# Attention over pairs of heads: VectorE copies turned rows two steps later

## The reference, cut to what matters

```
# "fox" half, per head: causal softmax with a decay added to the logits
logits = q k^T * scale + cum_q - cum_k
p = masked_softmax(logits, causal);  o = p @ v
# "latent" half, per head: softmax over the keys that an index picked
p = masked_softmax(logits, valid);   o = p @ c_sel
```

## Time and profile before

| what | value |
|---|---|
| median of 3 runs | 1916.68 us (1914.93 to 1918.02) |
| profiled execution, its own time | 1919.38 us |
| its span from first to last instruction | 1917.6 us |
| mean granted TensorE clock | 0.988 |
| PE busy | 1839.3 us (96% of the span) |
| DVE busy | 1027.5 us (54%) |
| ACT busy | 828.2 us (43%) |
| POOL busy | 592.6 us (31%) |
| the loop of the change | about 808 to 892 us of the span |

### The profile page before, as it was taken

The page is one execution under the profiler, slowest core; times in us unless marked ns, Lnnn a source line. Parts: engine busy times, 40 slices in busy tenths (PEclk is TensorE's granted clock), DMA queues, the critical chain, the costliest instruction groups (busy, mean ns, idle before and its releaser), DMA issues.

```text
span 1917.6 us, 27389 instructions
## 1 busy us (share of the span) xinstructions
PE 1839.3 (96%) x10554; PEld 1451.5 (76%) x10554; DVE 1027.5 (54%) x2006; ACT 828.2 (43%) x1569; POOL 592.6 (31%) x421
## 2 busy tenths in 40 slices
PE   8999999997888999999999999999999999999998
PEld 7878889842223778767888888889888888888886
DVE  3170442521111869663477676842577725767677
ACT  4123651311111543375554544353377655444543
POOL 4344431011110233356322223233055643232221
PEclk9999999999999999999999999999999999999999
DMA  7223404699999412121132223222203012233321
GB/s 236 98 94 118 140 1 154 251 392 419 420 420 370 167 45 88 46 88 35 54 132 88 88 88 120 98 94 67 45 2 89 2 44 88 88 131 108 113 88 45
DMA packets 86867, 252.06 MB, mean 131 GB/s; under 512 B 12212, under 2 KB 19700, under 8 KB 74448
## 3 DMA queue, kind: packets, MB, share of 16 engines
q1 hardware_dynamic: 81344, 238.79, 33.9%
q0 software_dynamic: 4592, 9.30, 1.3%
q10 hardware_dynamic: 800, 2.20, 0.3%
HBM read 241.89 MB, written 15.73 MB: 134 GB/s over the span
## 4 chain that ended last, share of the span: by engine, by line
PE 86%; DVE 4%; DMA 4%; ACT 3%; issue 2%; POOL 0%; ACTq 0%; DVEq 0%; POOLq 0%
PE psA L1606 42%; PE psS L2054 4%; PE psA L1649 3%; DMA ring<-in_w_down_e 3%; PE psA L2018 2%; PE psO L2352 2%; PE psO L1836 2%; PE psT L1836 2%; PE psS L1836 2%; PE psT L2402 2%; DVE x L3089 2%; DMA big<-in_w_down_e 1%; PE psA L1471 1%; PE psA L1785 1%; PE psS L1649 1%
## 5 line engine op out<-in xcount | busy, mean ns | idle before, releaser
L1290 POOL TENSOR_TENSOR w_slot<-ring,w_slot 128x1024 fp32r<-128x1024 f32 (+1 forms) x81 | 214.0, 2656 | 524.7 <-ACT w_slot L2433 524.4
L1606 PE MATMUL psA<-hT_hi,w_slot 128*128 128x512 f32 x960 | 298.2, 390 | 0.0
L2433 ACT ACTIVATE w_slot<-ring 128x1024 fp32r<-128x1024 f32 (+2 forms) x183 | 196.8, 1086 | 164.4 <-DVE ring L3089 75.0
L1606 PEld LDWEIGHTS psA<-hT_hi,w_slot 128*128 128x128 f32 x960 | 180.4, 188 | 37.3
L1606 PE MATMUL psA<-hT_lo,w_slot 128*128 128x512 f32 x480 | 187.0, 390 | 0.0
L3089 DVE TENSOR_TENSOR w_slot<-ring,w_slot 128x1024 fp32r<-128x1024 f32 x98 | 119.9, 1225 | 115.7 <-ACT w_slot L2433 115.7
L3089 DVE TENSOR_TENSOR x<-psA,x 128x512 f32<-128x512 f32 (+1 forms) x186 | 117.1, 662 | 104.2 <-PE psA L1606 68.8
L1606 PE MATMUL psA<-w_slot,hid_part 128*128 128x512 f32 x672 | 161.4, 390 | 0.0
L2433 ACT ACTIVATE big<-psA 128x512 f32<-128x512 f32 (+6 forms) x134 | 61.7, 482 | 208.7 <-PE psA L1606 126.0
L1606 PEld LDWEIGHTS psA<-w_slot,hid_part 128*128 128x128 f32 x672 | 126.2, 188 | 26.1
L2433 ACT ACTIVATE scr<-scr,stat 128x384 f32<-128x384 f32 (+3 forms) x224 | 123.7, 555 | 19.1 <-DVE stat L4079 9.8
(11 more groups left out here) (557 smaller groups left out, 4450.2 us busy)
## 6 DMA issues: line engine op xcount, KB each, us to landing
ring<-in_mlp_w SPq DMA_DIRECT2D x32, 2048.0 KB, 8.1
ring<-in_w_in SPq DMA_DIRECT2D x8, 2048.0 KB, 8.1
ring<-in_w_gate_e SPq DMA_DIRECT2D x14, 1024.0 KB, 16.3
ring<-in_w_up_e SPq DMA_DIRECT2D x14, 1024.0 KB, 20.7
ring<-in_w_down_e SPq DMA_DIRECT2D x13, 1024.0 KB, 28.3
big<-in_w_down_e SPq DMA_DIRECT2D x12, 1024.0 KB, 26.4
ring<-in_ab_w_in SPq DMA_DIRECT2D x5, 2048.0 KB, 8.6
scr<-in_w_down_e SPq DMA_DIRECT2D x7, 1024.0 KB, 27.0
```

The costliest lines, as they stand in the source:

```text
L1290: nc.gpsimd.tensor_tensor(part(w_lo, c), raw_piece(c), part(w_hi, c).bitcast(F32), ALU.subtract)\
L1606: ins = pe.matmul(o, a, b, start=(at == 1), stop=(at == 3 * len(terms)))
L2433: return nc.scalar.activation(o, i, f, **kw)
```

## The change

DVE copies item i - 8 at odd step i, where it copied item i - 6. The copy stays behind the maximum and the reciprocal of its step. So between the turn of an item and its copy DVE now does both maxima of the next pair and their step's reciprocal, too. No instruction is added or taken away, and ACT's, PE's and POOL's orders stay as they are.

```
--- before.py
+++ after.py
@@ -3937,7 +3937,7 @@
                             scalar=3e38, op0=ALU.add, op1=ALU.min, accum_out=negm[:, col:col + 1]).then_inc(p_masked, 1)
                     if 2 <= i < n_pairs and i % 2:
                         weigh_pair(i)
-                    k = i - TURN_LAG - 1
+                    k = i - TURN_LAG - 3
                     if 0 <= k < n_pairs and k % 2:
                         dve.wait_ge(p_turned, k + 1)
                         if k >= TURNED:
```

## The result

The changed kernel is slower: 1932.64 us median (1931.17 to 1933.81, 4 runs) against 1917.35 us (1914.93 to 1918.14, 4 runs) on the same chip. The ratio is 1.0081, its 95% interval 1.0064 to 1.0099. That is 15.3 us more, where 11.1 were forecast: inside the stated range, but above the forecast's own range of 8.0 to 13.5 added.

A forecast was written before the change was run, and what follows sets the result against it. PE was taken to bound the loop, DVE costing only where PE waits for it. Terms 9.0 + 1.1 + 0.6 + 0.4 = 11.1 us on the 1916.7 us median gave 1927.8 us, range 1923 to 1933.

The forecast's parts named there:

- the forecast's own range: Whole kernel: 8.0 to 13.5 us added to the median, so 1924.7 to 1930.2 us; the forecast had 80%.
- What bounds the kernel: Loop: PE sets the end; DVE's 25.8 us of waits cost nothing by themselves, PE's 1.4 us for copies matter.
- The wait moves to the maximum: DVE in the loop: the first maximum waits for the same turn through its 7-row ring, so the wait stays.
- Item 7's term: Behind item 7's turn (512 columns): PE's next turn comes 1.29 us later in 7 places, 9.0 us.
- Items 3 and 5: Behind their turns, latent half only: 0.27 and 0.14 us lost, four times each, 1.1 and 0.6 us.
- The rival in which the fox half hides the loss: Loop: the turn stalls in the latent half alone, 6.9 us added, 1923.6 us; chance 6%.
- The clock: Loop: PE's stalls make its clock fall, 1.7 us each; three falls taken, 1932.9 us; chance 7%.
- The range: Whole kernel: 1923 to 1933 us, from the stall in the latent half alone to three falls of the clock.
- The rule on VectorE: Item 7's maxima: the next operation waits for an empty pipeline, 1.1 us more in seven places; not counted.
- No change: Behind the loop: the delay is taken up later by a PE wait, 1916.7 us; chance 4%.
- faster: Loop: maxima reach ACT and POOL 0.6 us earlier, PE's waits of 5.0 and 1.4 vanish, 1910.3 us; chance 3%.

The follow-up runs named there:

- The run with eight rows: The changed kernel with 8 instead of 7 SBUF rows for the masked scores: 1922.74 us against 1916.56 before, ratio 1.0030.
- the swap: The changed kernel with a maximum's two waits in the other order, first the turn, then the scores: 1930.24 us against 1916.56 before, ratio 1.0068.
- the filled kernel: The changed kernel with TensorE repeating the narrow pair's scores three times in six steps: 1928.26 us against 1916.56 before, ratio 1.0065.
- the kernel before, filled: The kernel before the change with the narrow pair's scores repeated three times in the same six places: 1918.90 us against 1916.51, ratio 1.0011.

## Why the prediction was right in its mechanism and short in its size

**What bounds the kernel** was right. DVE's 25.8 us of waiting were worth nothing, and PE's 1.4 us were the line to follow. The loss went through to the end: the loop's 15.5 us and the median's 15.3 agree. How often the clock fell in the loop of the timed runs isn't known, so the agreement is good to a fall or two (1.6 us each).

**The wait moves to the maximum** was right: 34.3 us now stand at L3935. The run with eight rows shows that it is the ring of 7 rows that puts it there.

**Item 7's term** (7 x 1.29 = 9.0) was right from the release on, 2.13 us as worked out. It missed 0.11 us ahead of the release, in T itself. I set the maximum's start equal to the copy's, but the maximum waits for two semaphores, the later one last, and starts 0.11 later than the copy did. That is 0.11 in each of 15 places, 1.6 us; the swap took 1.5 us from the loop beside the clock. **Items 3 and 5** (0.27 and 0.14) show the same: PE waits 0.30 and 0.16 there, and the whole latent cycle grew from 8.63 to 887.92 - 877.35 = 10.57 us, so by 1.94 for 1.70 forecast. The fox cycle grew from 831.60 - 821.75 = 9.85, release to release, to 831.21 - 819.95 = 11.26, so by 1.41, where 1.29 + 0.11 is 1.40. The rival in which the fox half hides the loss is out. The sum without the clock would have been 11.1 + 1.6 = 12.7; the runs give 12.3.

**The clock** was the step that failed in weight. I gave it 7% as a rival beside the forecast, on the ground that PE stays much busier here (8.3 of 10.3 us) than around the stalls of the earlier trace rows. That ground failed: the first fall came in a stretch of 8.63 busy us in 10, behind one wait of 1.37 us. It fell twice in the profiled execution, 3.2 us, and these were at nothing in the sum; 11.1 + 1.6 + 3.2 = 15.9, for 15.5 measured. That the falls come from the idle time rests on the kernels side by side: the filled kernel has none, nor has any kernel with shorter waits. Its price for one fall (1.7 us) was good: 1.6 here. The rule of the Trainium skill that I cited (TensorE: Matmul & The Clock Gate, A second HAM failure mode: psum-queue depth-cycling) is borne out by these runs (a granted clock of 0.83, then 0.93 and 0.90, where the loop stood at 1.00 before), and I should have given it more weight, since I weighed it against stalls of 0.34 us in the loop, and the stalls of my own forecast (1.29 us more) were up to five times as long.

**The range** held by luck as much as by the sum. The forecast by itself ended at 1930.2, and the measured 1932.64 lies beyond it. It is inside the stated 1923 to 1933 only because I had stretched that to the rival's three falls, 5.1 us; in their place came two falls and the hand-over, 3.2 + 1.6 = 4.8 us.

The rule on VectorE (VectorE: DVE Perf Modes, The DRAIN you can't avoid) would not have given the right time here either, in the half of it that I cited: 877.97 - 877.35 = 0.62 and 878.58 - 877.97 = 0.61 between starts for instructions of 0.69. The same section adds that a next instruction which is not held starts earlier, and that is what these rows show.

**No change** and **faster** are out. POOL's scaling did come earlier (PE's loads wait 1.0 us for it instead of 5.0), and as forecast that gave nothing back.

## What to carry to other kernels

Before a consumer is moved behind other work in an in-order queue, ask what that other work waits for: here the two maxima waited for the very turn whose copy was put behind them, so the move didn't hide a wait but added 1.3 us of work between two dependent steps of the bounding engine. The cost then shows only where that engine has little else to do, and one item in four made four fifths of it. And idle time on TensorE can be dearer than its length: behind some of the stalls of 1.4 to 1.7 us the clock came down here, so their price is worked out with a fall or two of 1.6 us.

## What the hardware showed that I had not expected

- The order of two semaphore waits matters: with the wait that ends last written second, the maximum starts 0.12 us later than with that wait written first (0.78 and 0.66 us from the turn's first matmul). In both kernels the trace shows the wait written second as a semaphore instruction of its own (L3934, 57 and 58 times).
- The clock fell in the loop of the three kernels whose stalls reached 1.6 to 1.7 us (two falls, one, one). Each of them has four such places in the latent half, two of 1.3 to 1.4 us in the fox half and one of 1.1 to 1.2 us at the end; three of the falls came behind 1.6 to 1.7 us, one behind 1.37. A second profile of the kernel with the waits swapped has one fall as well, at the same place. In the six other changed kernels and the kernel before, where the longest stall is 1.2 us, it never fell in the loop. Which of the places brings a fall, the runs don't tell.
- Matmuls repeated with the same shape into the same banks cost less each than a few alone: in the kernel before, filled, twelve rows of repeats and four of the real scores took 1.10 us together, where the four alone take 0.42. Why, the runs don't tell.
